# Two layers of a streaming encoder on one Trainium2 core: the projections of the sample's 64 tokens as two column products instead of one

## The reference, cut to what matters

```python
def hybrid_mixer(h, ...):
    proj = h @ w_in                      # (tokens, 1024) @ (1024, 2376)
    q, k, v, iq, ik, iw, u = jnp.split(proj, SPLIT_POINTS, axis=-1)   # 512, 128, 128, 512, 64, 8, 1024 columns
    ...                                  # rotary, indexer scores, top-k, attention; conv branch from u
def trunk_layer(x, c, ...):
    h = rms_norm(x, g_norm_mix) * (1 + sc_a) + sh_a
    mix, new_state = hybrid_mixer(h, ...)
    x = x + gt_a * (mix @ w_out)         # (tokens, 1024) @ (1024, 1024)
    h = rms_norm(x, g_norm_ffn) * (1 + sc_f) + sh_f
    x = x + gt_f * hierarchical_moe(h, ...)   # top-2 of 16 experts
```

## Time and profile before

| | |
|---|---|
| runs, median of 3 | 1450.54 us |
| profiled execution | 1449.31 us |
| its span | 1447.5 us |
| mean granted TensorE clock | 0.914 |
| PE busy | 1253.6 us, 87% |
| PE weight loads | 733.4 us, 51% |
| DVE / ACT / POOL busy | 39% / 25% / 11% |
| HBM traffic | 200 GB/s over the span |

### The profile page before, as it was taken

How to read it: one execution, slowest core, us unless ns; L and a number is a source line. 1 busy time by engine, 2 the same in 40 slices (tenths; PEclk the granted TensorE clock), 3 DMA queues, 4 the chain that set the end, 5 groups by cost and what they waited for, 6 DMA issues and landing times.

```text
span 1447.5 us, 16324 instructions
## 1 busy us (share of the span) xinstructions
PE 1253.6 (87%) x6291; PEld 733.4 (51%) x6291; DVE 569.4 (39%) x1478; ACT 368.4 (25%) x861; POOL 152.4 (11%) x218
## 2 busy tenths in 40 slices
PE   4898699987889998999837989899686999999990
PEld 0452254543545586777523533454345457777760
DVE  1227689123236531111107257980323455111115
ACT  2214120035741111111114133001468111111111
POOL 0312050010000150000020113200100011000002
PEclk7899899997999999999967989899858999999995
DMA  9428997260960479999953120224121016799985
GB/s 362 133 69 324 352 341 228 82 228 5 313 230 30 160 211 386 356 369 365 325 184 115 59 71 30 65 67 137 35 56 25 0 68 221 252 365 361 369 289 210
DMA packets 136887, 283.95 MB, mean 196 GB/s; under 512 B 11581, under 2 KB 91877, under 8 KB 130409
## 3 DMA queue, kind: packets, MB, share of 16 engines
q1 hardware_dynamic: 116128, 208.66, 42.7%
q0 software_dynamic: 8352, 42.50, 8.5%
q10 hardware_dynamic: 12329, 31.74, 6.2%
HBM read 236.86 MB, written 52.40 MB: 200 GB/s over the span
## 4 chain that ended last, share of the span: by engine, by line
PE 69%; DVE 11%; DMA 7%; ACT 6%; issue 3%; SPq 2%; ACTq 1%; POOLq 0%; POOL 0%; DVEq 0%
PE ps L508 44%; PE ps L813 9%; PE ps L518 5%; PE ps L671 3%; DMA W<-in_w_gate 3%; PE ps L732 3%; ACT arena L1194 2%; SPq L419 2%; DMA X<-in_x_sample 2%; DVE arena L1498 2%; PE ps L859 2%; DVE small L1497 1%; DVE arena L1537 1%; DVE arena L1588 1%; PE ps L632 1%
## 5 line engine op out<-in xcount | busy, mean ns | idle before, releaser
L508 PE MATMUL ps<-W,arena 128*128 128x256 f32 (+1 forms) x1280 | 348.1, 428 | 10.3 <-DMA W<-in_w_up 5.2
L508 PEld LDWEIGHTS ps<-W,arena 128*128 128x128 f32 x1280 | 242.2, 193 | 85.4 <-issue 49.9
L508 PE MATMUL ps<-W,hT 128*128 128x512 f32 (+3 forms) x480 | 195.0, 563 | 9.7 <-DVE gt L1369 6.6
L518 PE MATMUL ps<-C,arena 128*128 128x128 f32 (+3 forms) x835 | 118.4, 282 | 55.6 <-DVE arena L1417 18.1
L813 PE MATMUL ps<-W,hT 128*128 128x512 f32 (+1 forms) x320 | 144.7, 606 | 5.7 <-ACT hT L1251 5.7
L518 PEld LDWEIGHTS ps<-C,arena 128*128 128x128 f32 (+3 forms) x835 | 95.6, 148 | 96.6 <-issue 36.1
L508 PEld LDWEIGHTS ps<-W,hT 128*128 128x128 f32 (+1 forms) x480 | 87.4, 186 | 110.3 <-issue 83.4
L508 PE MATMUL ps<-hT,W 128*128 128x128 f32 (+1 forms) x512 | 129.4, 414 | 7.1 <-ACT arena L1118 7.1
L508 PEld LDWEIGHTS ps<-hT,W 128*128 128x128 f32 x512 | 79.1, 193 | 58.4 <-issue 50.5
L1805 DVE TENSOR_TENSOR arena<-arena,ps 128x256 f32<-128x256 f32 x32 | 13.5, 421 | 221.7 <-ACT arena L1292 221.7
L813 PEld LDWEIGHTS ps<-W,hT 128*128 128x128 f32 (+1 forms) x320 | 57.1, 183 | 79.9 <-issue 73.6
(11 more groups left out here) (250 smaller groups left out, 1174.1 us busy)
## 6 DMA issues: line engine op xcount, KB each, us to landing
W<-in_w_ada SPq DMA_DIRECT2D x48, 1024.0 KB, 7.4
W<-in_w_gate SPq DMA_DIRECT2D x32, 1024.0 KB, 10.6
W<-in_w_up SPq DMA_DIRECT2D x32, 1024.0 KB, 13.1
W<-in_w_down SPq DMA_DIRECT2D x32, 1024.0 KB, 7.8
y_d<-arena ACTq DMA_DIRECT2D x33, 512.0 KB, 7.3
W<-in_w_in SPq DMA_DIRECT2D x16, 1024.0 KB, 8.5
arena<-x_d SPq DMA_DIRECT2D x31, 512.0 KB, 11.5
arena<-arena SPq DMA_DIRECT2D x128, 79.2 KB, 2.1
```

What stands on the lines that cost most here:

```text
L508: ins = T.matmul(out, l, r, start=n == 0, stop=n == len(pairs) - 1, skip_group_check=True)
L518: count(T.transpose(o, i, ident[0:m, 0:m]), done if n == len(outs_ins) - 1 else None)
```

## The change

For tile 4 alone, each step's `T.matmul` becomes two, with the same stationary operand (64 tokens) and one part of the weight columns each. The first writes to partitions 0 to 63 of the bank and the second to partitions 64 to 127. Tiles 0 to 3 keep their products. ACT and DVE read the two halves from the two sets of partitions. For c = 1 the parts are 200 columns (values, indexer key and weights) and 128 (keys), with ACT's five copies as before; for c = 0 and c = 2 two parts of 256 columns and two ACT copies in place of one; for each half of the output projection two parts of 256 columns and two DVE multiplies by the gate in place of one.

```diff
+            def products_by_side(bank, k_pairs, done=None, before=None, halfway=None):
+                for n, (lhs, sides) in enumerate(k_pairs):
+                    if before is not None and n == len(k_pairs) // 2:
+                        before()
+                    for side, rhs in enumerate(sides):
+                        ins = T.matmul(bank[64 * side:64 * side + DEC, 0:rhs.shape[-1]], lhs, rhs, start=n == 0,
+                                       stop=n == len(k_pairs) - 1, skip_group_check=True)
...
+                    count(ins, done if n == len(k_pairs) - 1 else None)
...
-                    products(ps[job % 3][0:rows_of(t), 0:n], [(hT[:, k, tokens(t)], wv[k // 4][:, k % 4, :]) for k in range(KC)], L["proj"],
-                             before=midway, halfway=us[0] % 6 if last else None)
+                    if t == 4:
+                        sides = ((P, n), (0, P)) if c == 1 else ((0, 2 * P), (2 * P, n))
+                        products_by_side(ps[job % 3], [(hT[:, k, tokens(t)], [wv[k // 4][:, k % 4, c0:c1] for c0, c1 in sides]) for k in range(KC)],
+                                         L["proj"], before=midway, halfway=us[0] % 6 if last else None)
...
-                            ins = T.matmul(ps[5 + n % 3][0:rows_of(t), :], hT[:, 4 * q + k, tokens(t)], wv[:, k, :],
-                                           start=q == 0 and k == 0, stop=last, skip_group_check=True)
+                            sides = [(0, 512)] if t < 4 else [(0, 256), (256, 512)]
+                            for side, (c0, c1) in enumerate(sides):
+                                ins = T.matmul(ps[5 + n % 3][64 * side:64 * side + rows_of(t), 0:c1 - c0], hT[:, 4 * q + k, tokens(t)],
+                                               wv[:, k, c0:c1], start=q == 0 and k == 0, stop=last, skip_group_check=True)
...
+                    side = [b[64 * a:64 * a + DEC, 0:2 * P] for a in range(2)]
+                    if t == 4 and c == 0:
+                        for a in range(2):
+                            ins = S.copy(iqr[0:m, t, 4 * a:4 * a + 4, :], side[a].rearrange("p (h d) -> p h d", d=HD))
...
+                    elif t == 4:
+                        for a in range(2):
+                            ins = S.copy(qkr[0:m, t, a:8:2, :], side[a].rearrange("p (i d) -> p i d", d=HD))
...
+                    if t < 4:
+                        ins = V.tensor_tensor(wtmp[:, n % 2, :], ps[5 + n % 3][:, :], gate, ALU.mult)
+                    else:
+                        for side in range(2):
+                            cs = slice(256 * side, 256 * side + 256)
+                            ins = V.tensor_tensor(wtmp[0:m, n % 2, cs], ps[5 + n % 3][64 * side:64 * side + DEC, 0:256], gate[:, cs], ALU.mult)
```

More of the change, by code:

```diff
@@ L512, in products @@
                     count(ins, done if n == len(pairs) - 1 else None)
+            def products_by_side(bank, k_pairs, done=None, before=None, halfway=None):
[5 more added lines that the diff above has]
+                                       stop=n == len(k_pairs) - 1, skip_group_check=True)
+                    if halfway is not None and n == len(k_pairs) // 2:
+                        assert not done_units
+                        done_units.append(halfway)
+                    count(ins, done if n == len(k_pairs) - 1 else None)
             def turn(outs_ins, done):
@@ L587, in project @@
                         came(us[0])
-                    products(ps[job % 3][0:rows_of(t), 0:n], [(hT[:, k, tokens(t)], wv[k // 4][:, k % 4, :]) for k in range(KC)], L["proj"],
-                             before=midway, halfway=us[0] % 6 if last else None)
+                    if t == 4:
[3 more added lines that the diff above has]
+                    else:
+                        products(ps[job % 3][:, 0:n], [(hT[:, k, tokens(t)], wv[k // 4][:, k % 4, :]) for k in range(KC)], L["proj"],
+                                 before=midway, halfway=us[0] % 6 if last else None)
                     if last:
@@ L1024, in out_of @@
                     act.wait_ge(L["proj"], job + 1)
-                    if c == 0:
+                    side = [b[64 * a:64 * a + DEC, 0:2 * P] for a in range(2)]
+                    if t == 4 and c == 0:
+                        for a in range(2):
+                            ins = S.copy(iqr[0:m, t, 4 * a:4 * a + 4, :], side[a].rearrange("p (h d) -> p h d", d=HD))
+                    elif t == 4 and c == 1:
+                        for q in range(2):
+                            S.copy(iqr[0:m, t, 8 + q, :], side[0][:, P:P + HD])
+                        S.mul(iw[0:m, t, :], side[0][:, P + HD:P + HD + 8], IW_SCALE)
+                        S.copy(qkf[0:m, t, 512:640], side[1][:, 0:P])
+                        ins = S.copy(vrow[0:m, t, :], side[0][:, 0:P])
+                    elif t == 4:
+                        for a in range(2):
+                            ins = S.copy(qkr[0:m, t, a:8:2, :], side[a].rearrange("p (i d) -> p i d", d=HD))
+                    elif c == 0:
                         ins = S.copy(iqr[0:m, t, 0:8, :], b[0:m, :].rearrange("p (h d) -> p h d", d=HD))
@@ L1654, in gated @@
                         dve.wait_ge(L["xadd"], n - 1)
-                    V.tensor_tensor(wtmp[0:m, n % 2, :], ps[5 + n % 3][0:m, :], gt[0:m, t // 4, hf * 512:hf * 512 + 512],
-                                    ALU.mult).then_inc(L["wod"], 1)
+                    gate = gt[0:m, t // 4, hf * 512:hf * 512 + 512]
+                    if t < 4:
+                        ins = V.tensor_tensor(wtmp[:, n % 2, :], ps[5 + n % 3][:, :], gate, ALU.mult)
+                    else:
+                        for side in range(2):
+                            cs = slice(256 * side, 256 * side + 256)
+                            ins = V.tensor_tensor(wtmp[0:m, n % 2, cs], ps[5 + n % 3][64 * side:64 * side + DEC, 0:256], gate[:, cs], ALU.mult)
+                    ins.then_inc(L["wod"], 1)
                     xs = X[0:m, t, hf * 512:hf * 512 + 512]
```

## The result

The changed kernel took 1434.19 us, the median of 4 runs (1430.32 to 1435.08), and the kernel before 1450.13 beside it. The ratio is 0.988, with a 95% interval from 0.985 to 0.990. So it is faster by 16 us, 6 us above the forecast of 1428: inside the stated range of 1422 to 1438, but outside the 1425 to 1432 that the forecast's own working allowed. In a second comparison it took 1435.53 against 1449.55: 0.992, from 0.988 to 0.995. By the two ratios 18 and 12 us of the forecast 22.8 arrived.

The account below looks back on a forecast made before the run. PE was taken as the bound (87% busy, 69% of the chain), priced stage by stage. Per layer 4.7 + 3.1 + 3.6 = 11.4 us, 22.8 in two, gave about 1428 from 1450.54; own range 1425 to 1432, with rivals 1422 to 1438.

Parts of the forecast that it names:

- The value products: Attention's two 64-column products on one bank, overlapping in pairs; taken as the law for tile 4: 3.69 us in place of 6.87.
- The fixed remainder: Added to the paired records' time in each split product: about 0.19 us in the value products, 0.13 of it fixed.
- no overlap: Rival, 3%: in tile 4's products 32 records take 6.91 us where 16 took 6.87; 1451 us, no change.
- slower: Rival, 3%: the second product's weight load waits for the first's matmul; 1.41 us per step, about 1490 us.
- a fixed cost per added matmul: Rival, 8%: 52 ns paid on each of 160 added records; 8.3 us go, 1436 us.
- The input projections' terms: Tile 4's projections: c = 0 and 1 gain 4.7 us a layer, c = 2 gains 3.1 a layer.
- swallowed by DVE: Rival, 10%: DVE's selection rounds in both layers' c = 2 hold their times; 6.2 us go, 1434 us.
- The output projection's term: Tile 4's output projection and routing: net gain 3.6 us a layer, bounds 2.0 and 3.8.
- The clock: Rival, 10%: layer 1's clock falls too, losing 2.6 to 3.3 us per stretch, 1431 to 1435; without layer 0's fall, 1424 to 1425.
- a start that is 11 us earlier moves them as a block: Experts: weight loads and rows move up with the earlier start, so nothing is lost there; start near 511 us.
- The prediction's own sign of being wrong: Products, PE's wait, conv and expert starts and expert step come as forecast, yet the span doesn't fall by 20 us.

Follow-up runs that it names:

- same_half: Changed kernel with both column products of tile 4 on partitions 0 to 63, side by side in the bank: 1452.11 us, ratio 1.0018 to the kernel before.
- only_c2: Kernel before with only projection c = 2 of tile 4 split: 1442.47 us, ratio 0.9954 to the kernel before.
- only_out: Kernel before with only the output projection of tile 4 split: 1449.78 us, ratio 1.0002 to the kernel before.
- late_loads: Changed kernel with layer 1's small loads, issued by POOL in layer 0, moved behind the scatters into the experts: 1437.62 us, ratio 0.9910 to the kernel before.
- kept_busy: Changed kernel plus matmuls of constants, results unread, where PE would wait for DVE around the output projection: 1425.63 us, ratio 0.9839 to the kernel before.
- after_again: The changed kernel once more, for a second profile and comparison: 1435.53 us, ratio 0.9916 to the kernel before.
- kept_busy_late: Changed kernel with both the edits of kept_busy and late_loads: 1427.64 us, ratio 0.9843 to the kernel before.
- no_out: Changed kernel with the output projection as before, c = 0, 1 and 2 split: 1431.93 us, ratio 0.9895 to the kernel before.

## Why the prediction was right, and where it failed

**The overlap held.** The value products gave 3.69 us for 8 steps and 2.95 for c = 1; measured were 3.60 and 2.88. The fixed remainder was put 0.07 to 0.09 us too high. `same_half` shows the mechanism by its absence. With that the rivals *no overlap* and *slower* fall, and so does *a fixed cost per added matmul*: at 52 ns for each of its 16 added records, a product would have taken 3.69 + 0.83 = 4.5 us. `same_half` has 0.18 us for 16 added records, 11 ns each. The Trainium skill's page TensorEngine Tiling (Array Packing), section Instruction Overhead, puts about 60 cycles on each matmul. Added in full to each record, as the prediction had it (an estimate of 25 ns at 2.4 GHz), that is more than twice the 11 ns. The page's own example is that a matmul with one column takes as long as one with 60; read so, as a floor for narrow matmuls, it says nothing against these records of 256 columns.

**The input projections' terms held**: for c = 0 and 1, 9.4 us in both layers were forecast and 8.8 measured (by the ratio); for c = 2, 6.2 and 6.7. The rival *swallowed by DVE* falls too: 1434 us was its figure as well, but `only_c2` gains at least 3 us of the 6.2 that it would have taken. The first conv starts at 229.90, 6.3 us earlier and not 7.8. The difference lies in the scores stage of layer 0, which takes about 1.5 us longer in five of the 14 profiles than in the others, among both those with the split of c = 0 and 1 and those without; why is open.

**The output projection's term failed.** The step as it was put: "They start at about 488.45: a gain of 2.1, with PE idle for a microsecond", and "Net 3.6 a layer; bounds 2.0 ... and 3.8". In the order of things it was right: PE waits 1.29 us there, and a kernel whose clock is kept gets 3.6. But the sum was made at full clock on both sides of a wait that it had itself introduced. The shortened products open or lengthen three waits for DVE in a stretch of 13.4 us: 1.29, 0.65 and 1.66 us in place of 0.73. Behind them, in each of the eight layers of `only_out`, `late_loads` and the two profiles of the changed kernel, the 32 records of `first_rows` run mostly at the 1.2 GHz level (5.4 to 5.8 us in place of 3.84). In seven of the eight the two opening records do too (2.07 against 1.12), and in four the steps right behind `turn_h`. That is the rival *The clock*, with 10% for 1431 to 1435. It named the place and nearly the price, 2.6 to 3.3 us in each such stretch; measured against `kept_busy`, the slow rows cost 4.3 us in layer 0 and 2.9 in layer 1. The lower bound of this term should have been 0 or a little below, and since the earlier trace rows already had a fall behind a 0.73 us wait in one layer of two, the rival deserved far more than 10%.

The Trainium skill's page TensorE: Matmul & The Clock Gate, Part 1 (The HAM clock gate), says that the slow level is the default, that activity releases it and that idle time brings it back. The rows agree, with one addition: here no single wait is longer than 1.7 us, and one of 0.73 us was enough in the earlier trace rows.

**The experts' start failed in part.** "a start that is 11 us earlier moves them as a block": the stage of layer 0 got 3.4 us longer in the profiled pair. A later step is 11.44 us long as before. PE's waits for expert weights in that stage vary between kernels from 3.4 to 11.1 us, and no experiment tied them down.

**The sum.** 22.8 forecast; `kept_busy` has 23.3 at 1450, with all four terms in place. The changed kernel has 12 to 18: the missing 5 to 10 us are the output projection's 7.2, of which its two profiles show the clock as the taker, and a remainder (conv, the start of the experts) that is no larger than what these stages vary between profiles. The prediction's own sign of being wrong was a span that doesn't fall by 20 us while the products take 3.6 us: they did, and it fell by 14.3 (the conv of layer 0, expected near 228.5 us, came at 229.90, and the experts, expected near 511, at 514.71). It named the experts' weight loads as the likeliest taker; the clock took more. So the time fell into the range because the range had been widened for the rivals, among them the one that came true; the working itself, with its 1425 to 1432, was too hopeful by one term.

## What to carry to other kernels

A product with 64 stationary columns can be cut into two column products, written to the two halves of a bank's partitions and issued in turns. Here 256 and 256 columns took 3.60 us in place of 6.87, and 200 and 128 took 2.88 in place of 4.48, doubled weight loads included: price them by the pairs, at the pace of the wider part, and check that what follows can use it. When a shortened piece of TensorE's work leaves it waiting for another engine, price the work behind the wait at both clock levels; several short waits near one another brought the clock down far more often than one. Matmuls that nobody reads can pay where such waits can't be removed (useful work moved into them was tried, and gave no difference clear of noise): here 4.2 us of filler a layer made the kernel 10 us faster, while the same filler where TensorE hardly waited made it 4 to 7 us slower.

## What the runs showed of the hardware

- Filler in waits: `kept_busy` adds ten matmul instructions in two layers (20 records) and is faster than `after_again` by 0.8% (the ratios 0.9839 and 0.9916); on one chip, `kept_busy_late` is faster than `late_loads` by 0.7%.
- Three waits of 1.29, 0.65 and 1.66 us within 13.4 us were followed by a granted clock of 0.57 to 0.60 in both layers of the changed kernel, and by slow rows in 8 of 8 layers; one of 0.72 us was followed by 1.00 in `no_out`, in both layers, and one of 0.73 by 0.53 in layer 0 of the kernel before, 1 of 10 layers with a single wait.
- Twice as many records on the same half, half as wide, cost 0.18 us a product of 8 steps: 7.05 against 6.87.
